# PSUM banks handed out by the scheduler, and a fixed order for the opening's loads, in a pool-and-attention block on 8 cores

## The reference, cut to what matters

```
mod_x = silu(c) @ mod_w + mod_b                      # sh1, sc1, g1, sh2, sc2, g2
hc = modulate(rms_norm(ctx), csh1, csc1);  kc, vc = hc @ w_in[:, k | v columns]
h  = modulate(rms_norm(x), sh1, sc1)
q, k = rope(rms_norm(heads(h @ wq))), rope(rms_norm(heads(h @ wk)));  v = h @ wv
attn = window_attention(q, k, v, kc, vc, sink)       # 3 blocks of 128 keys and 256 context keys
mix  = (sigmoid(..) * (attn @ w_attn_proj) + sigmoid(..) * (pool(h) @ w_pool_proj)) @ w_out
x1 = x + g1 * mix
out = x1 + g2 * ((silu(h2 @ w_a) * (h2 @ w_b)) @ w_down),  h2 = modulate(rms_norm(x1), sh2, sc2)
```

## Time and profile before

| | us |
|---|---|
| median of 3 runs | 1055.45 |
| lowest, highest of them | 1054.94, 1177.26 |
| the profiled execution | 1056.16 |
| its span on core 0, the slowest | 1054.6 |
| spans of the eight cores | 1046.4 to 1054.6 |
| busy in the span: PE, DVE, ACT, POOL | 989.3, 514.4, 476.7, 211.7 |

### The profile page before, as it was taken

How to read it: one execution, slowest core, us unless ns; L and a number is a source line. 1 busy time by engine, 2 the same in 40 slices (tenths; PEclk the granted TensorE clock), 3 DMA queues, 4 the chain that set the end, 5 groups by cost and what they waited for, 6 DMA issues and landing times.

```text
span 1054.6 us, 15129 instructions; the slowest of 8 cores (1046.4 to 1054.6 us)
## 1 busy us (share of the span) xinstructions
PE 989.3 (94%) x6206; PEld 465.1 (44%) x6206; DVE 514.4 (49%) x925; ACT 476.7 (45%) x639; POOL 211.7 (20%) x239
## 2 busy tenths in 40 slices
PE   1577897999999999999999999999999999999998
PEld 0334453544444444455444444444444444444443
DVE  3489977776656656553247642124322135321244
ACT  2478876687988788663228841110011100111100
POOL 0231433655334547211210000000000000000000
PEclk9689988999999999999999999999999999999999
DMA  9986746733444547903760034220042220022034
GB/s 233 297 244 149 121 74 108 124 57 58 75 63 60 89 62 110 171 1 69 260 170 1 1 72 78 40 41 0 10 83 39 40 40 1 3 38 41 1 145 174
DMA packets 24502, 90.80 MB, mean 86 GB/s; under 512 B 2672, under 2 KB 3568, under 8 KB 20976
## 3 DMA queue, kind: packets, MB, share of 16 engines
q0 software_dynamic: 16416, 53.71, 30.9%
q1 hardware_dynamic: 8016, 36.11, 9.7%
HBM read 135.14 MB, written 8.39 MB: 136 GB/s over the span
## 4 chain that ended last, share of the span: by engine, by line
PE 86%; DMA 6%; DVE 5%; ACT 2%; issue 1%; POOL 0%; SPq 0%; DVEq 0%; POOLq 0%
PE psall L1320 29%; PE psall L1046 18%; PE psall L1334 14%; PE psall L1249 5%; PE psall L650 5%; PE psall L838 4%; PE psall L884 4%; PE psall L941 3%; DMA m1f<-mod 2%; DMA xstc<-ctxT 2%; DVE pT L856 1%; DMA m2w<-mod 1%; PE psall L779 1%; PE psall L898 1%; ACT pT L851 1%
## 5 line engine op out<-in xcount | busy, mean ns | idle before, releaser
L1320 PE MATMUL psall<-h2T,wu 128*128 128x512 bf16 x1408 | 304.7, 379 | 0.0
L1320 PEld LDWEIGHTS psall<-h2T,wu 128*128 128x128 bf16 x1408 | 137.8, 98 | 166.1
L1323 ACT ACTIVATE sil<-psall 128x512 f32<-128x512 f32 x88 | 52.5, 597 | 338.6 <-PE psall L1320 338.5
L1324 DVE TENSOR_TENSOR actT<-psall,sil 128x512 bf16<-128x512 f32 x88 | 60.9, 692 | 234.3 <-PE psall L1320 228.4
L851 ACT ACTIVATE pT<-psall 128x1024 bf16<-128x1024 f32 x160 | 158.0, 1023 | 18.8 <-PE psall L838 17.8
L1334 PE MATMUL psall<-actT,wd 128*128 128x512 bf16 x704 | 152.4, 379 | 0.0
L1337 DVE SCALAR_TENSOR_TENSOR xacc<-psall,dotc,xacc 128x512 f32<-128x512 f32 x96 | 72.1, 751 | 80.1 <-PE psall L1334 80.1
L1334 PEld LDWEIGHTS psall<-actT,wd 128*128 128x128 bf16 x704 | 68.9, 98 | 83.0
L1046 PE MATMUL psall<-hall,rg 128*128 128x512 bf16 x320 | 75.6, 379 | 0.6 <-ACT csc L1068 0.6
L425 POOL DMA_DIRECT2D wu<-w_up_p x22 | 11.8, 534 | 282.6 <-PE psall L1320 280.4
L856 DVE TENSOR_TENSOR pT<-pT,cmt 128x1024 bf16<-128x1024 bf16 x64 | 59.6, 932 | 15.8 <-ACT pT L851 15.6
(11 more groups left out here) (186 smaller groups left out, 1274.7 us busy)
## 6 DMA issues: line engine op xcount, KB each, us to landing
rg<-w_c POOLq DMA_DIRECT2D x60, 256.0 KB, 4.0
wu<-w_up_p POOLq DMA_DIRECT2D x22, 512.0 KB, 5.0
m1f<-mod SPq DMA_DIRECT2D x8, 1024.0 KB, 30.0
m2w<-mod POOLq DMA_DIRECT2D x16, 512.0 KB, 7.0
xacc<-xT SPq DMA_DIRECT2D x4, 2048.0 KB, 8.6
out<-xacc SPq DMA_DIRECT2D x32, 256.0 KB, 2.1
cw<-w_c POOLq DMA_DIRECT2D x6, 768.0 KB, 19.8
xsta<-xT SPq DMA_DIRECT2D x2, 2048.0 KB, 12.1
```

The lines of the kernel that those rows point to most:

```text
L1320: T.op("pe", lambda e, k=k, ab=ab: e.matmul(ps[bs + ab], lhsT=wu[us][:, ab, k, :], rhs=h2T[:, k, cc * 512:(cc + 1) * 512], start=(k == 0), ...
L1323: T.op("act", lambda e: e.activation(out=sil[si][:], in_=ps[bs], func=AF.Silu), reads=[PS(bs)], writes=[slk], tab="si")
L1324: T.op("dve", lambda e: e.tensor_tensor(out=actT[:, fi, cc * 512:(cc + 1) * 512], in0=ps[bs + 1], in1=sil[si][:], op=ALU.mult), reads=[PS( ...
```

## The change

It has four parts.

1. **Banks.** From the attention on, a group that needs a bank for filler work, for a PV half or for a transpose asks `T.bank()` and gets a `Bank` without a number. `forward` keeps a list of spare banks (4 to 7, from `T.share_banks`), gives one out when such a group is first placed on PE, and takes it back when its last reader has been placed; while none is spare such groups can't be placed. After the last pass the numbers are filled in, and the waits on the earlier user of each bank with them. Copies take their PSUM operand late (`lambda: ps[b]`), since its number isn't known when they are emitted.
2. **Fixed sequence where scratch is shared.** The order that the fixed banks had given is written as explicit dependencies on PE: `tailop` (first matmul of a q or k unit behind the tail that reads the same scratch) and `transop` (first PV matmul behind the transposes that read the same `Otok`). `lastop` does the same in the merge, for `csc`.
3. **Opening.** While `T.lead` is true groups get a priority ahead of all others (`g - 1e6`): `fcon`, `ropf`, `xsta`, `m1f0` to `m1f7`, `cmt`, `wkv`, the memsets, silu, exp, `gbh`, and `make_rope(0)`, which moves up there; `make_rope(1)` follows at ordinary priority.
4. **`PASSES` from 12 to 40.**

```diff
-PASSES = 12
+PASSES = 40
...
+    def share_banks(self, banks):
+        for b in banks:
+            st = self.state[("ps", b)]
+            self.pool0.append((b, ([st["w"]] if st["w"] is not None else []) + list(st["r"])))
+
+    def bank(self):
+        v = Bank(len(self.vbanks))
+        self.vbanks.append(v)
+        return v
...
         def late(g, e):
             x = self.groups[g][0].alts
-            return rt[g] + (x[e][2] if x and len(x[e]) > 2 else 0.0)
+            r = rt[g] + (x[e][2] if x and len(x[e]) > 2 else 0.0)
+            return max(r, min(spare)[0]) if g in self.vneed else r
...
+            if g in self.vneed:
+                fit = [x for x in spare if x[0] <= t + 1e-9]
+                it = max(fit) if fit else min(spare)
+                spare.remove(it)
+                held[self.vneed[g]] = it[1]
+                extra.append((g, it[1], it[2]))
...
+            for v in self.gbanks.get(g, ()):
+                uses[v] -= 1
+                if uses[v] == 0:
+                    spare.append((max(done_t[h] for h in self.vusers[v]), held[v], v))
...
-            cur = self.forward(preds, succ, [-x for x in tail], TABWAIT)
+            cur = self.forward(preds, succ, [g - 1e6 if g in self.first else -x for g, x in enumerate(tail)], TABWAIT)
...
+    T.lead = True
     dma("sp", fcon[:], fcond, ("fcon",), "fcon")
...
+    make_rope(0)
+    T.lead = False
+    make_rope(1)
...
     def fbank():
-        bank["fb"] += 1
-        return bank["lo"] + bank["fb"] % (8 - bank["lo"])
+        return T.bank()
...
+            if j == 0 and si in tailop:
+                o.deps.add(tailop[si].idx)
...
-            ob = 4
+            ob = T.bank()
...
+                    if r == ki == 0 and ui % 2 in transop:
+                        o.deps.add(transop[ui % 2].idx)
...
-            tpv = ps[4].bitcast(BF16)
+            tb = T.bank()
+            tpv = lambda: ps[tb].bitcast(BF16)
```

More of the change, by code:

```diff
@@ L45, in __init__, with __getitem__ @@
         self.sb = False
+class Bank:
+    __slots__ = ("n", "ops", "idx")
+    def __init__(self, idx):
+        self.n, self.ops, self.idx = None, [], idx
+class Banks:
+    def __init__(self, aps):
+        self.aps = aps
+    def __getitem__(self, i):
+        return self.aps[i.n if isinstance(i, Bank) else i]
 class Trk:
@@ L66, in __init__ @@
         self.bias = 0
+        self.first = set()
+        self.vbanks = []
+        self.pool0 = []
+        self.lead = False
     def tile(self, off, shape, dtype, name):
@@ L118, in op @@
             deps.update(st["r"])
+        for k in list(reads) + list(writes):
+            if k[0] == "ps" and isinstance(k[1], Bank):
+                k[1].ops.append(o.idx)
         deps.discard(o.idx)
@@ L130, in op @@
             self.prio.append(g + self.bias)
+            if self.lead:
+                self.first.add(g)
         self.groups[g].append(o)
@@ L135, in op, with end_share @@
         return o
+    def share_banks(self, banks):
[6 more added lines that the diff above has]
+        return v
+    def end_share(self):
+        for b, _ops in self.pool0:
+            st = self.state[("ps", b)]
+            for v in self.vbanks:
+                st["r"].extend(v.ops)
     def final_wait(self, eng, sems):
@@ L146, in forward @@
         free = {e: 0.0 for e in self.ENG}
+        done_t = [0.0] * ng
+        uses = [len(x) for x in self.vusers]
+        held = {}
+        spare = []
+        wait0 = []
+        for b, gs in self.pool0g:
+            wait0.append([b, gs, len(gs)])
+            if not gs:
+                spare.append((0.0, b, None))
+        extra = []
         wire = 0.0
@@ L175, in forward @@
             for e in self.ENG:
-                if not ready[e]:
+                cand = ready[e] if spare else [g for g in ready[e] if g not in self.vneed]
+                if not cand:
                     continue
-                now = [g for g in ready[e] if late(g, e) <= free[e]]
+                now = [g for g in cand if late(g, e) <= free[e]]
                 if now:
@@ L203, in forward @@
             order.append(g)
+            done_t[g] = done
+            for v in self.gbanks.get(g, ()):
+                uses[v] -= 1
+                if uses[v] == 0:
+                    spare.append((max(done_t[h] for h in self.vusers[v]), held[v], v))
+            for w in wait0:
+                if g in w[1]:
+                    w[2] -= 1
+                    if w[2] == 0:
+                        spare.append((max(done_t[h] for h in w[1]), w[0], None))
             for h in succ[g]:
@@ L209, in forward, with backward @@
                         ready[e2].append(h)
-        return end, order, start, used, took
-    def backward(self, preds, succ, start, used, took):
+        return end, order, start, used, took, extra
+    def backward(self, preds, succ, start, used, took, extra):
         ng = len(self.groups)
+        preds = [set(x) for x in preds]
+        for g, b, v in extra:
+            preds[g].update(self.vusers[v] if v is not None else self.pool0d[b])
+        succ = [[] for _ in range(ng)]
+        for g in range(ng):
+            preds[g].discard(g)
+            for h in preds[g]:
+                succ[h].append(g)
         left = [len(x) for x in succ]
@@ L418, in build_program @@
     psall = nc.alloc_psum_tensor("psall", [128, 4096], F32)
-    ps = [psall[:, i * 512:(i + 1) * 512] for i in range(8)]
+    ps = Banks([psall[:, i * 512:(i + 1) * 512] for i in range(8)])
     def PS(i):
@@ L430, in tt_any, with copy_any @@
         T.op(None, None, reads=reads, writes=writes, alts={"dve": (f, cd, slow), "pool": (f, cp)}, sb=True)
-    def copy_any(out, in_, reads, writes, ca, cd):
+    def copy_any(out, in_, reads, writes, ca, cd, late=False):
         T.op(None, None, reads=reads, writes=writes, alts={
-            "act": (lambda e: e.activation(out=out, in_=in_, func=AF.Copy), ca),
-            "dve": (lambda e: e.tensor_copy(out=out, in_=in_), cd)})
+            "act": (lambda e: e.activation(out=out, in_=in_() if late else in_, func=AF.Copy), ca),
+            "dve": (lambda e: e.tensor_copy(out=out, in_=in_() if late else in_), cd)})
     def flat(t):
@@ L900, in tail @@
             T.op("dve", lambda e: e.tensor_copy(out=qc[:, 4 * jj:4 * jj + 4, q0:q0 + 128],
-                                                in_=tpv[:, 0:512].rearrange("p (r q) -> p r q", r=4)),
-                 reads=[PS(4)], writes=[("qT%d" % (n // 4), 4 * jj + r, n % 4) for r in range(4)], cost=0.42)
+                                                in_=tpv()[:, 0:512].rearrange("p (r q) -> p r q", r=4)),
+                 reads=[PS(tb)], writes=[("qT%d" % (n // 4), 4 * jj + r, n % 4) for r in range(4)], cost=0.42)
@@ L1045, in mm @@
             for k in range(nk):
-                T.op("pe", lambda e, k=k: e.matmul(ps[b], lhsT=lf(k), rhs=rf(k), start=(k == 0), stop=(k == nk - 1)),
-                     reads=wkk + kf(k), writes=[PS(b)], inc=(k == nk - 1))
+                o = T.op("pe", lambda e, k=k: e.matmul(ps[b], lhsT=lf(k), rhs=rf(k), start=(k == 0), stop=(k == nk - 1)),
+                         reads=wkk + kf(k), writes=[PS(b)], inc=(k == nk - 1))
+                if k == 0 and sx in lastop:
+                    o.deps.add(lastop[sx].idx)
+            return o
         def hr(k):
```

63 lines of the change are left out of this document (42 added, 21 removed).

## The result

After took 1064.05 us in the median of 4 runs (1063.01 to 1064.91), before 1055.2 beside it. The ratio is 1.0083, 95% interval 1.0067 to 1.0099. I had forecast 1045.1 and a gain of 10.4; the time rose by 8.8. The loss is less than the 2% that I had called the least a measurement can tell, but many times the width of this interval.

A forecast was written before the change was run, and what follows sets the result against it. PE was taken as nearly full from 200 us on, fixed from 490, with gains in the head and five places: −1.5 − 1.4 − 1.4 − 2.0 − 4.1 = −10.4, so 1045.1 us beside the median; range 1036 to 1056.

The forecast's parts named there:

- E: 200 to 490 us: with two banks PV's second half no longer waits for bank 4; −4.1 us (bounds −4.7, +1.0).
- D: 120 to 200 us: two PE pauses, waits for m2w and half clock behind them; −2.0 us (gain to 12, loss to 9).
- A: The opening's tail: chunk 0's last modulation ends at about 52 in place of 54; gain 1.5 us (bounds 0, 2.9).
- up to 2 us come back: In the opening: wq0 issued up to 2 us later, halo and chunk 1 queued behind it, giving back up to 2 us.
- B: Halo squares' matmul at 73.98 us could start at 72.54 with a bank given at first use; gain 1.4 (0 to 3.0).
- C: 76 to 91 us: PV, modulation and score work put ahead of chunk 1's first projection; −1.4 us (bounds −3.0, +1.6).
- Rival 3: Slower: m2w reloads come too late and PE waits; 1059 us, or 1062 with the qT multiply held up; chance 0.10.
- The fixed block: From 490 us to the end: PE busy 561.46 of 565.00 us at full clock, so nothing changes there.
- if fillers wait for banks: Sign that the prediction is wrong: filler groups, now sharing four banks with PV and transposes, wait for a bank.

The follow-up runs named there:

- e1: Order of after unchanged, but bank numbers given out anew, the spare bank free longest in place of the last-freed; 1060.4 us, ratio 1.0043.
- e10: After with order and banks unchanged, each multiply or addition on POOL waiting for the end of the one before; 1060.65 us, ratio 1.0047.
- e11: Order of after with both the oldest spare bank (e1) and the gaps between POOL's instructions (e10); 1056.72 us, ratio 1.0014.
- e2: After with the scheduler itself giving out the bank free longest, so the order changes as well; 1054.71 us, ratio 0.9987.
- e18: The kernel before, order and banks unchanged, with gaps between POOL's instructions alone; 1056.84 us, ratio 1.001.
- e14: e2 with the load of wq0 issued on modulation columns 5 in place of 6, the halo's four rotary products behind it; 1056.98 us, ratio 1.0003.

## Why the prediction was wrong, by its own steps

**E is the step that failed.** Its first half was right: PV's wait went from 4.1 to 0.4. The upper bound of +1.0 for fillers that "may wait for a bank" was not. I took it from the longest old wait, as if a bank that is handed out were handed out as early as before. I had the rule `max(fit)` in front of me and priced only how many banks there are, not which one is given. What the runs showed in its place: the merge's matmuls wait 9.3 for banks, and behind the longest of these waits PE runs at half clock, which I had counted in D and not in E. The steady part came out 10.0 longer, not 4.1 shorter. Of these 10.0, by e1 2.6 are the choice of bank and by e10 5.5 are a stop of DVE beside POOL that now reaches PE, with its half clock; both together give 8.2 (e11). What is left to e2, 332.7 − 328.8 = 3.9, is its order, and e2 ends 2.1 below before.

**The stops were in the trace of before, and I cost them at nothing.** DVE's 3.81 for a mask multiply stood beside a median of 0.69 in the same group. I used POOL's effect on DVE only for L556 in the opening. The runs show that the stops aren't new: the 64 mask multiplies take 17.3 us more than 64 of the shortest in before, 21.7 in after and 8.4 in e2 (11.3 for before, in what was expected of e18, is too low). What is new is that PE waits for what stands behind the longest.

**A was half right.** The last modulation of chunk 0 ended at 49.8 on core 0 in place of 54.0 (forecast: about 52), and the last k and v step 1.9 us earlier in the median over the cores (54.4 to 52.5), where I had 1.5 to 2.1. The two small transfers ahead moved the landing of the last `m1f` tile by 0.2 (45.1 to 45.3, medians), not by the estimated 1. The part that I called "up to 2 us come back" was 5.8: the first score went from 75.9 to 79.8, though the chunk ended earlier. I priced the later issue of `wq0` (46.7 in place of 43.8) and not that it then takes longer to land, 12.5 in place of 10.9: it landed 4.5 later, at 59.2 in place of 54.7. The reload of `xsta`, whose issue moved ahead (49.8 in place of 52.7), is in flight beside it; that this is the reason isn't shown. That `wq0` isn't the whole of it is shown by e14.

**B and C.** The wait for bank 6 is gone from the list: the halo's squares (L609) now wait 1.1 for ACT's root, which is where B said that they could start. But all of it stands 2 to 4 later, so nothing of B is seen in the time. C's place didn't come earlier: on core 0 the first k projection of chunk 1 begins at 96.21 in place of 90.61, at half clock as before (3.37 for eight). C had ACT as what comes last there. In after it is DVE, on core 0:

```profile
90.08 4.81 DVE xstb L621 x8
...
95.36 0.55 PE L1215 MATMUL psall<-csil,m2w 128*128 128x2 bf16 x16 [2.42 <-DVE ta L737]
96.21 3.37 PE L748 MATMUL psall<-hall,wkv 128*128 128x512 bf16 x8 [0.30 <-DVE Otok L995]
```

Eight multiplies of chunk 1 (`xstb`) stand on DVE ahead of `ta`, which has to read its bank before the modulation block can have it: a wait of 2.4 for a bank, and the projection needs the same eight. The stretch behind it is shorter all the same: from the first score to the merge after needs 121.4 in place of 127.0, which may be the work put ahead. A to D together were to give 6.3 by 200 us; the merge began 1.7 earlier (202.9 to 201.2).

**D.** The waits for m2w, 3.9 on core 0 and 0.8 to 3.3 on the others, are gone in after on seven cores; core 1 has 3.0. The granted clock of 120 to 200 on core 0 rose from 0.89 to 0.96. That is the better of the two sides of D; its size can't be read apart from the rest of that stretch. Rival 3, the slower one, had the right sign of the total and the wrong place: no reload cost more than 1.7, and behind POOL's three reloads in a row PE has no wait for `qT`.

**The fixed block** was fixed: 518.0 and 517.9.

What came true was named only as a sign ("if fillers wait for banks") and as E's bound of +1.0. It belonged among the rivals, with a price of its own.

## What to carry to other kernels

When a scheduler with modelled times hands out a shared buffer, it should give the one that has been free longest: the last-freed one leaves no slack for errors of the model, and here that one line cost 0.4% at an unchanged order and 1.0% with the order that came of it (e2). A short wait that is removed by sharing a private resource must be weighed against every user of the resource, with the worst lateness of its readers, and the longest instance of a group (here 4.6 us against a median of 0.69) tells this lateness, not its mean. A wait of some microseconds also has to be priced with the half clock behind it. A simulated order that is a little better than another need not be so on the chip: by the simulated clock after ends at 1065.2 and e2 at 1066.9, and on the chip e2 is 0.96% faster. A change that moves the order is judged by experiments with the order held.

## What the runs showed of the hardware

A two-input multiply on DVE stood still for as long as POOL ran two-input instructions back to back: 4.58 us over four of them in after, 3.81 over four in before, 2.42 over two (a case at 246.11 of before, shown here), each time ending about 0.6 after the last:

```profile
245.67 1.28 POOL L429 TENSOR_TENSOR mg0a<-csc,csc 128x512 bf16<-128x512 f32 x1
...
246.11 2.42 DVE L856 TENSOR_TENSOR pT<-pT,cmt 128x1024 bf16<-128x1024 bf16 x1
246.90 1.06 POOL L429 TENSOR_TENSOR sab<-sab 128x525 f32<-128x525 f32 x1
```

It isn't slowed by a share, as the scheduler's factor of 1.6 has it, but stopped until POOL leaves a gap. On core 0 all 12 mask multiplies of before that took over 1 us, and all 21 of after, end 0.54 to 0.57 after the end of a POOL instruction. A gap made by a wait of POOL on its own last instruction let it in (e10: 2.4 at most). In six cases of before the multiply began first; it then took its usual 0.66 to 0.69, and POOL's instruction could be the one that took longer, here 1.62 where the median of its kind is 1.27:

```profile
155.38 0.68 DVE L856 TENSOR_TENSOR pT<-pT,cmt 128x1024 bf16<-128x1024 bf16 x1
155.58 1.62 POOL L429 TENSOR_TENSOR qT<-ta,sroot 128x512 bf16<-128x512 f32 x1
```

The Trainium skill, page "GPSIMD Engine Reference", section "8. Key points", says that POOL shares its SBUF interfaces with VectorE and that they contend where a DVE instruction has two SBUF inputs or runs in a 2-port mode. The trace agrees: the multiply has two inputs in SBUF and took 4.58 in place of 0.69.
